# Two of four weight sums ahead of the gating in each feed-forward block, and four moves of order, in a hand-ordered fp32 kernel of two transformer blocks

## The chip, the cores and the metric

The kernel runs on one core of a Trainium2 chip. The metric is the device time of one launch in microseconds, measured on the chip. All inputs, weights and outputs are fp32; TensorE runs its matmuls on fp32 data.

## What is computed

Batch 1, 256 tokens, width 1024. The first block is a swiglu feed-forward (2816 wide, added with a gate and a factor of a half), a mixer of differential attention and an mLSTM, and a second swiglu feed-forward. The second block is a gated deltanet layer (8 heads of 128), then a layer of native sparse attention (NSA, 16 heads of 64) on keys and values shared across heads, and a last norm. Each stage is modulated by columns computed from a vector c. Cut to what matters here:

```python
def swiglu(u, w_gate, w_up, w_down):
    return (jax.nn.silu(u @ w_gate) * (u @ w_up)) @ w_down

# first block, after ada modulation of each norm:
h = h + FFN_RES * gt1[:, None, :] * swiglu(u, w1_gate[l], w1_up[l], w1_down[l])
...
q = jnp.einsum('bshd,hde->bhse', xch, w_mq)      # mLSTM
k = jnp.einsum('bshd,hde->bhse', xch, w_mk)
...
merged = jax.nn.sigmoid(ga) * (ya @ w_proj_a[l]) + jax.nn.sigmoid(gb) * (yb @ w_proj_b[l])
h = h + gt2[:, None, :] * (merged @ w_out[l])
...
h = h + FFN_RES * gt3[:, None, :] * swiglu(u, w2_gate[l], w2_up[l], w2_down[l])

# gated deltanet layer:
k = l2norm(k)                                    # sums of squares over 128 channels
decay = jnp.where(incl, jnp.exp(jnp.where(incl, diff, 0.0)), 0.0)

# NSA layer:
s_c = jnp.einsum('bghqd,bgcd->bghqc', qb, k_cmp).astype(jnp.float32) + dense_bias(d_c)
y = jnp.sum(gates[..., None].astype(o.dtype) * o * jax.nn.silu(z), axis=2)
```

## The kernel before, in words

The kernel is one program written by hand, `build()`, with one function for each engine (`tensor`, `vector`, `scalar`, `gpsimd` and one for SyncE). No scheduler sets the order: each function lists the steps of its engine in the order in which the engine runs them, and the engines meet by counting semaphores. `pe.up(name)` counts a result of TensorE under a name and `pe.at(name)` waits for it; `dve`, `act`, `pool` and a set for the transfers work in the same way. A `Ring` is a set of buffers used in turn: `open` gives the next buffer with what has to be waited for before it is written, `close` says which result frees it. PSUM has eight banks; in most stages banks 0 to 2 form the ring L, 3 and 4 the ring S and 5 to 7 the ring X. Weights come through the ring W of four slots in SBUF, fetched by SyncE in the order in which its function lists them.

All arithmetic lines of the profile are those of thin helpers: L189 matmul, L192 transpose, L195 activation (ScalarE), L198 tensor_tensor, L201 tensor_scalar, L204 scalar_tensor_tensor, L207 the custom multiply-and-sum, L222 memset, L225 DMA. So a row is told from another by its engine, its shape and the names of its tiles: `slots` are weights, `arena` is a large common region, `U`, `ABT`, `tmpA` and `x` are activations or sums over them, `tmps` are small buffers, `ps` is PSUM, `mods` are the modulation columns.

**The feed-forward blocks.** Gate and up weights come in blocks of 256 columns, 0 to 10. Blocks 5 to 10 of the first feed-forward (f1) and 1 to 10 of the second (f2) are done with seven products of half size in the place of eight (Strassen's scheme, Winograd's form), which needs sums over the weights, over the activations and over the results. `v_t(e, f, b)` (L1043) makes four sums t1 to t4 over the weights of block b on VectorE. `t_gu` (L1057) runs the products on TensorE in the order p1, p2, p6, p5, p7, p3, p4; p6 and p5 want t2 and a sum over activations, p7 wants t3 and the bank that ScalarE's copy u2 empties. ScalarE (`s_gu_blocks`, L3743) runs for block b: the copy s1 of block b, the tanh of block b - 1, and the copies u2, s5, u3, c21 of block b. The tanh waits for VectorE's sums of results of block b - 1, which are made by `v_gu` (L1132: c1 and c22). `v_gu_act` (L1151) does the gating of a block: two instructions that turn the tanh and the two results into the activation that the down projection reads, and free the rings EG and XG of two buffers each. `v_gu_blocks` (L3444) sets VectorE's order: the gating of block b - 1, the four sums of block b + 1, chunks of modulation, the sums of results of block b. In block 10 there are no weight sums left; the sums over gated values (`v_sd`) and the first sums of the down projection stand there.

**Chunks of modulation.** Modulation columns are made on VectorE by a multiply-and-sum over rows that come in chunks of 128 by 1024 into the ring AR of four buffers. `v_ada_chunks` runs one instruction for each chunk, and the table `CHUNKS` (L485) says how many chunks are taken in which block; SyncE's fetches follow the same table.

**The gated deltanet layer.** TensorE sums the squares of keys in rows; ScalarE's `s_qk_rows` (L2294) copies the rows out of PSUM into `tmps`, TensorE transposes them (L192) and sums on. `s_d_exp` runs the exponentials of the decay of a group of heads, two instructions of 256 and two of 128 columns for each group, behind VectorE's sums of a bias row that comes by DMA.

**The NSA layer.** Before the loop over scores, `t_linear` makes z for n = 0 and 1 in banks of L (each is turned into a silu by ScalarE and VectorE's scalar_tensor_tensor). In the loop, z halves use the ring LZ of two banks and scores the ring PS of four. TensorE waits before the loop for the bank of L that PS takes over, and inside it for the bank that LZ takes over.

**The bias rows.** `p_bias_rows` (L1313) on GpSimd spreads the rows of the bias over 128 copies in DRAM, in two transfers of 1536 KB. They are read in the NSA layer. In the `gpsimd` function they stand before the rotations of q and k (`p_rotate`), behind the wait for the first product of xm 1, one of the seven-product units of the mixer's input projection (in their order: xm 1, va, ga, gb, op, then pa and pb, the projections `w_proj_a` and `w_proj_b`). `p_ml_in` brings gate rows of the mLSTM, `p_merge` adds the two branches.

## Time and profile before

| | |
|---|---|
| median of 3 runs | 1186.77 us (1186.38 to 1187.87) |
| the profiled execution's own time | 1185.74 us |
| its span on the core | 1183.9 us |
| granted clock of TensorE, mean | 0.998 of full speed |
| TensorE, matmuls in flight | 1167.5 us (99%) |
| TensorE, weight loads | 1078.0 us (91%) |
| VectorE | 737.2 us (62%) |
| ScalarE | 351.4 us (30%) |
| GpSimd | 85.3 us (7%) |
| moved by DMA | 241.78 MB, mean 204 GB/s |

The span is what the profiler saw of the core from the first to the last instruction; the time of the same run is 1.8 us longer. TensorE has two rows: PE, the matmuls, and PEld, the weight loads that run beside them. In both a row groups instructions of one kind that follow one another, with the idle time before the first of them in brackets and what ended it. An idle engine costs time only where TensorE waits for it.

### The profile page before, as it was taken

Reading aid. Unit: us, or ns where it says so; the run is one execution under the profiler, and the core shown is the slowest. Engines: PE = TensorE matmul, PEld = TensorE weight load, DVE = VectorE, ACT = ScalarE, POOL = GpSimd, SP = SyncE. Lnnn points to the kernel's source line nnn. Section 1 sums busy time; section 2 is a strip of 40 time slices with the busy share of each in tenths; the row PEclk is TensorE's granted clock in tenths of the full one; section 3 lists DMA queues with packets and bytes.
Section 4 is the critical chain, followed back from the end, with each engine's and each line's share of the span. In section 5 each row is a group of like instructions: output and inputs, shape, how many; then the busy total and the mean of one; then the engine's idle time right before and its main releaser. Section 6 shows DMA issues by size and latency. Waiting matters only on the chain.

```text
span 1183.9 us, 21320 instructions
## 1 busy us (share of the span) xinstructions
PE 1167.5 (99%) x8862; PEld 1078.0 (91%) x8862; DVE 737.2 (62%) x1658; ACT 351.4 (30%) x996; POOL 85.3 (7%) x104
## 2 busy tenths in 40 slices
PE   9999999999999999999999999999999999999997
PEld 7889999998878999999999999988888998888887
DVE  4458888576048866972898878467845231167632
ACT  2111110232133555212321210245323431056542
POOL 0000000200011000021000000310004010000111
PEclk9999999999999999999999999999999999999999
DMA  9968949884555454677599739574524643642311
GB/s 343 363 214 302 331 145 303 291 307 148 202 192 186 151 214 175 223 264 234 168 362 312 269 132 302 182 269 158 142 64 143 214 143 113 194 127 73 113 66 37
DMA packets 164272, 241.78 MB, mean 204 GB/s; under 512 B 14033, under 2 KB 112559, under 8 KB 164176
## 3 DMA queue, kind: packets, MB, share of 16 engines
q1 hardware_dynamic: 156256, 230.45, 57.5%
q10 hardware_dynamic: 6784, 5.74, 1.6%
q0 software_dynamic: 1136, 4.22, 1.0%
q8 instruction: 70, 1.15, 0.4%
q14 instruction: 26, 0.21, 0.1%
HBM read 236.82 MB, written 4.62 MB: 204 GB/s over the span
## 4 chain that ended last, share of the span: by engine, by line
PE 85%; DVE 8%; DMA 3%; ACT 2%; issue 1%; POOL 0%; DVEq 0%; SPq 0%; ACTq 0%
PE ps L189 83%; DVE arena L198 3%; PE ps L192 2%; DMA slots<-in_w_mk 1%; DVE x L198 1%; DVE tmps L204 1%; ACT U L195 1%; DVE arena L207 1%; DMA slots<-in_w_proj_b 1%; ACT tmps L195 1%; DVE slots L198 0%; DMA bias_row<-rows 0%; DVE arena L204 0%; DVE slots L207 0%; ACT arena L195 0%
## 5 line engine op out<-in xcount | busy, mean ns | idle before, releaser
L189 PE MATMUL ps<-U,slots 128*128 128x128 f32 (+2 forms) x2800 | 478.9, 330 | 0.0
L189 PEld LDWEIGHTS ps<-U,slots 128*128 128x128 f32 (+1 forms) x2800 | 419.9, 190 | 40.5 <-issue 4.7
L189 PE MATMUL ps<-arena,slots 128*128 128x128 f32 (+1 forms) x1776 | 237.7, 294 | 0.9 <-DMA slots<-in_w_mk 0.9
L189 PEld LDWEIGHTS ps<-arena,slots 128*128 128x128 f32 x1776 | 225.4, 192 | 9.7 <-DMA slots<-in_w_mk 1.1
L195 ACT ACTIVATE tmps<-ps 128x256 f32<-128x256 f32 (+2 forms) x151 | 57.2, 382 | 342.6 <-PE ps L189 319.9
L207 DVE CUSTOM_DVE_ANT_0 arena<-arena,tmpA 128x1024 f32<-128x1024 f32 x96 | 118.0, 1272 | 17.0 <-DMA arena<-in_w_adaT 16.7
L195 ACT ACTIVATE arena<-ps 128x256 f32<-128x256 f32 (+3 forms) x150 | 59.3, 416 | 157.7 <-PE ps L189 153.9
L189 PE MATMUL ps<-arena 128*128 128x128 f32 (+7 forms) x940 | 101.9, 287 | 2.4 <-DVE arena L222 1.5
L189 PEld LDWEIGHTS ps<-arena 128*128 128x128 f32 (+2 forms) x940 | 92.5, 181 | 11.3 <-issue 3.7
L189 PE MATMUL ps<-ABT,arena 128*128 128x128 f32 (+5 forms) x752 | 81.9, 271 | 0.0
L189 PEld LDWEIGHTS ps<-ABT,arena 128*128 128x128 f32 (+3 forms) x752 | 72.5, 174 | 0.8 <-issue 0.8
L198 DVE TENSOR_TENSOR arena<-slots,arena 128x1024 f32<-128x1024 f32 (+1 forms) x44 | 58.6, 1331 | 0.6
L195 ACT ACTIVATE arena<-arena,st 128x128 f32<-128x128 f32 (+2 forms) x128 | 48.5, 403 | 35.2 <-DVE st L201 33.0
L189 PE MATMUL ps<-tmpA,slots 128*128 128x128 f32 x432 | 52.7, 275 | 0.0
L189 PEld LDWEIGHTS ps<-tmpA,slots 128*128 128x128 f32 x432 | 50.4, 192 | 0.0
L189 PE MATMUL ps<-x 128*128 128x128 f32 (+1 forms) x384 | 48.5, 284 | 0.6 <-DVE x L198 0.4
L204 DVE SCALAR_TENSOR_TENSOR tmps<-arena,hw,tmps 128x256 f32<-128x256 f32 x96 | 46.5, 485 | 3.4
L189 PEld LDWEIGHTS ps<-x 128*128 128x128 f32 x384 | 46.3, 192 | 1.8 <-DVE x L198 0.9
L189 PE MATMUL ps<-U,arena 128*128 128x128 f32 (+1 forms) x320 | 46.3, 296 | 0.0
L198 DVE TENSOR_TENSOR slots<-slots 128x1024 f32<-128x1024 f32 (+1 forms) x35 | 45.1, 1290 | 0.4
L195 ACT ACTIVATE U<-U,mods,sm 128x128 f32<-128x128 f32 (+1 forms) x72 | 30.3, 494 | 46.6 <-DVE sm L204 32.3
L189 PEld LDWEIGHTS ps<-U,arena 128*128 128x128 f32 x320 | 42.0, 192 | 1.6
(199 smaller groups left out, 1143.0 us busy)
## 6 DMA issues: line engine op xcount, KB each, us to landing
slots<-in_w_in SPq DMA_DIRECT2D x14, 2048.0 KB, 11.3
slots<-in_w_down SPq DMA_DIRECT2D x16, 1408.0 KB, 9.4
slots<-in_w_gate SPq DMA_DIRECT2D x18, 1024.0 KB, 8.5
slots<-in_w_up SPq DMA_DIRECT2D x18, 1024.0 KB, 11.1
arena<-in_w_adaT SPq DMA_DIRECT2D x36, 512.0 KB, 6.9
arena<-in_ada_w1T SPq DMA_DIRECT2D x24, 512.0 KB, 6.6
slots<-in_a_in_w SPq DMA_DIRECT2D x6, 2048.0 KB, 9.9
slots<-in_b_in_w SPq DMA_DIRECT2D x12, 1024.0 KB, 5.3
```

Of the source, the lines that this page charges most:

```text
L189: return Nothing() if self.e is None else self.e.matmul(*a, **k)
L192: return Nothing() if self.e is None else self.e.transpose(*a, **k)
L195: return Nothing() if self.e is None else self.e.activation(*a, **k)
L198: return Nothing() if self.e is None else self.e.tensor_tensor(*a, **k)
L204: return Nothing() if self.e is None else self.e.scalar_tensor_tensor(out=o, in0=i0, scalar=s, in1=i1, op0=op0, op1=op1)
L207: return Nothing() if self.e is None else self.e.tensor_tensor_reduce(*a)
```

## The change

Five edits, none of which adds or removes an instruction:

1. `v_t` takes a further argument `gated`. With it, the gating of that block is run between t2 and t3. `v_gu_blocks` passes block b - 1 while it makes the sums of block b + 1, so in blocks 6 to 9 of f1 and 2 to 9 of f2 the two gating instructions go from ahead of the four sums to between the second and the third. The first of the seven-product blocks has nothing to gate, and block 10 keeps its order.
2. The table `CHUNKS["f2"]` gives block 1 two chunks in the place of four, and block 9, which had none, two. The number of chunks is the same.
3. In the NSA layer the ring LZ takes banks 2 and 1 in the place of 2 and 0, and the ring PS bank 0 in the place of 1. The two waits follow.
4. ScalarE copies the rows of the keys' squares before the exponentials of the first group of decays, which stood ahead of it.
5. GpSimd issues the two copies of bias rows after the gate rows of the mLSTM, behind a wait for the first product of op 0, and no longer before the rotations.

```diff
--- before.py
+++ after.py
@@ -484,7 +484,7 @@
         AR = ring(*[arena[:, 5632 + 1024 * i:6656 + 1024 * i] for i in range(4)])
         CHUNKS = {"f1": {}, "f2": {}}
         for f, g0, counts in (("f1", 4, {4: 3, 5: 3, 6: 3, 7: 3, 8: 2, 9: 2}),
-                              ("f2", 18, {0: 3, 1: 4, 2: 3, 3: 3, 4: 3, 5: 3, 6: 3, 7: 3, 8: 3})):
+                              ("f2", 18, {0: 3, 1: 2, 2: 3, 3: 3, 4: 3, 5: 3, 6: 3, 7: 3, 8: 3, 9: 2})):
             n = 0
             for b, m in counts.items():
                 CHUNKS[f][b] = [(g0 + i // 4, i % 4) for i in range(n, n + m)]
@@ -1040,7 +1040,7 @@
             e.wait_ge(*dve.now())
             e.tensor_tensor(SU[3], a12, SU[1], ALU.subtract).then_inc(*dve.up("su", f))
 
-        def v_t(e, f, b):
+        def v_t(e, f, b, gated=None):
 
             t, free = TG.open(f, b)
             for x in free:
@@ -1050,6 +1050,8 @@
             e.tensor_tensor(t[:, 0], w[:, :, 0:4, P:T], w[:, :, 0:4, 0:P], ALU.subtract).then_inc(*dve.up(f, "t1", b))
             e.wait_ge(*dve.at(f, "t1", b))
             e.tensor_tensor(t[:, 1], w[:, :, 4:8, P:T], t[:, 0], ALU.subtract).then_inc(*dve.up(f, "t2", b))
+            if gated is not None:
+                v_gu_act(e, f, gated)
             e.tensor_tensor(w[:, :, 0:4, P:T], w[:, :, 4:8, P:T], w[:, :, 0:4, P:T], ALU.subtract).then_inc(*dve.up(f, "t3", b))
             e.wait_ge(*dve.at(f, "t2", b))
             e.tensor_tensor(t[:, 2], w[:, :, 4:8, 0:P], t[:, 1], ALU.subtract).then_inc(*dve.up(f, "t4", b))
@@ -2960,8 +2962,8 @@
 
 
         m15 = C("m15")
-        LZ = ring(banks[2][:, :], banks[0][:, :])
-        PS = ring(*[banks[b][:, :] for b in (3, 4, 5, 1)])
+        LZ = ring(banks[2][:, :], banks[1][:, :])
+        PS = ring(*[banks[b][:, :] for b in (3, 4, 5, 0)])
         EE = ring(B(0)[:, 0:816], B(0)[:, 816:1632], arena[:, 8 * UNIT + 1240:8 * UNIT + 2056], arena[:, 20384:21200])
         EA = ring(tmpA[:, :, :].rearrange("p i n -> p (i n)")[:, 0:1024], ABT[:, :, :].rearrange("p i n -> p (i n)")[:, 0:1024])
         ES = ring(*[st[:, i, :] for i in range(4)])
@@ -3402,12 +3404,12 @@
             t_cmp3(e, 1)
             for n in range(2):
                 t_linear(e, "z", n, U, u_in("n5"), 256, ("z", n))
-            for x in free_of(L, 1) + free_of(X):
+            for x in free_of(L, 0) + free_of(X):
                 e.wait_ge(*x)
             for t in range(10):
                 if t < 8:
                     t_na_scores(e, t)
-                for x in free_of(L, (2, 0)[t]) if t < 2 else ():
+                for x in free_of(L, (2, 1)[t]) if t < 2 else ():
                     e.wait_ge(*x)
                 if t < 9:
                     t_z_half(e, ZIN[t][0], 0)
@@ -3444,11 +3446,10 @@
         def v_gu_blocks(e, f, b0):
 
             for b in range(b0, 11):
-                if b > b0:
+                if b < 10:
+                    v_t(e, f, b + 1, b - 1 if b > b0 else None)
+                else:
                     v_gu_act(e, f, b - 1)
-                if b < 10:
-                    v_t(e, f, b + 1)
-                else:
                     v_sd(e, f, 0, 9)
                     v_dn_t1(e, f, 0)
                     v_dn_t2(e, f, 0)
@@ -3878,8 +3879,8 @@
             s_decay_in(e)
             s_conv(e, "dc", 15)
             s_qk_squares(e, 7)
+            s_qk_rows(e, "k", 7)
             s_d_exp(e, 0)
-            s_qk_rows(e, "k", 7)
             s_d_exp(e, 1)
             s_d_exp(e, 2)
             s_silu(e, "zg", 0)
@@ -3971,8 +3972,6 @@
         def gpsimd(e):
             p_bias(e)
             p_squares(e, "n2")
-            e.wait_ge(*pe.at("7", "p1", "xm", 1))
-            p_bias_rows(e)
             for pair in range(4):
                 p_rotate(e, "q", pair)
                 p_rotate(e, "k", pair)
@@ -3982,6 +3981,8 @@
                     for h in range(3):
                         p_ml_in(e, h)
             p_ml_in(e, 3)
+            e.wait_ge(*pe.at("7", "p1", "op", 0))
+            p_bias_rows(e)
             for b in range(2):
                 for half in range(2):
                     p_merge(e, b, half)
```

VectorE in the second feed-forward, from the chunks of block 1 on. The `L207` pairs are chunks, `tmps<-ps,tmps` and `tmps<-tmps,rstd` are the sums of results, `tmps<-tmps` and `arena<-tmps` the gating, and the rows with `slots` the weight sums t1 to t4. Before:

```order
L207 ISA arena,mods<-arena,tmpA 128x1024 [waits s_ada_chunk0]
L207 ISA mods 128x1
L207 ISA arena,mods<-arena,tmpA 128x1024 [waits s_ada_chunk1]
L207 ISA mods 128x1
L207 ISA arena,mods<-arena,tmpA 128x1024 [waits s_ada_chunk2]
L207 ISA mods 128x1
L198 TENSOR_TENSOR tmps<-ps,tmps 128x512 [waits s_products,s_scalar_results]
L198 TENSOR_TENSOR tmps<-tmps,rstd 128x2x128 [waits s_scalar_results]
L204 SCALAR_TENSOR_TENSOR tmps<-tmps 128x512 [waits s_scalar_results]
L198 TENSOR_TENSOR arena<-tmps 128x2x2x128 [waits s_vector_results]
L198 TENSOR_TENSOR arena<-slots 128x1024 [waits s_slot0,s_products]
L198 TENSOR_TENSOR arena<-slots,arena 128x1024 [waits s_vector_results]
```

Now:

```order
L207 ISA arena,mods<-arena,tmpA 128x1024 [waits s_ada_chunk0]
L207 ISA mods 128x1
L198 TENSOR_TENSOR tmps<-ps,tmps 128x512 [waits s_products,s_scalar_results]
L198 TENSOR_TENSOR tmps<-tmps,rstd 128x2x128 [waits s_scalar_results]
L198 TENSOR_TENSOR arena<-slots 128x1024 [waits s_slot0,s_products]
L198 TENSOR_TENSOR arena<-slots,arena 128x1024 [waits s_vector_results]
L204 SCALAR_TENSOR_TENSOR tmps<-tmps 128x512 [waits s_scalar_results]
L198 TENSOR_TENSOR arena<-tmps 128x2x2x128 [waits s_vector_results]
L198 TENSOR_TENSOR slots<-slots 128x2x4x128
L198 TENSOR_TENSOR arena<-slots,arena 128x1024
```

Two chunks are gone from ahead of the sums of results of block 1, and t1 and t2 of the next block stand ahead of the gating.

ScalarE in the gated deltanet layer, one piece of the difference (`arena<-arena,gates` are the exponentials, `tmps<-ps 128x128` is the copy of the rows):

```order
-L195 ACTIVATE arena<-arena,gates 128x256
-L195 ACTIVATE arena<-arena,gates 128x128
-L195 ACTIVATE arena<-arena,gates 128x256
-L195 ACTIVATE arena<-arena,gates 128x128
 L195 ACTIVATE tmps<-ps 128x128
+L195 ACTIVATE arena<-arena,gates 128x256
+L195 ACTIVATE arena<-arena,gates 128x128
+L195 ACTIVATE arena<-arena,gates 128x256
+L195 ACTIVATE arena<-arena,gates 128x128
```

The copy now stands ahead of the four exponentials of the first group.

GpSimd in the mixer, the end of its part, one piece of the difference (`arena<-tmps,arena` are rotations, `tmps<-blocks` the gate rows of the last head, `arena<-arena` the merges; the `+` row had stood ahead of the first rotation):

```order
 L198 TENSOR_TENSOR arena<-tmps,arena 128x512 x2
 L225 DMA tmps<-blocks 128x256
+L225 DMA bias_rows<-bias_row 128x8x384 x2
 L198 TENSOR_TENSOR arena<-arena 128x4x128 x4
 L225 DMA tmpA<-in_c_rows 128x1024
```

The two transfers of bias rows now follow the last gate rows and stand ahead of the merges.

## Rows read from the trace of the kernel before

**Rows 1.** The page: busy us (share of the span) and instructions of each engine.

```profile
PE 1167.5 (99%) x8862; PEld 1078.0 (91%) x8862; DVE 737.2 (62%) x1658; ACT 351.4 (30%) x996; POOL 85.3 (7%) x104
```

**Rows 2.** TensorE's waits by what ended them: us in total, times, longest.

```profile
PE ps L189 <- ACT tmps L195: 2.1, 2, 1.4
PE ps L189 <- DVE arena L222: 1.5, 1, 1.5
PE ps L192 <- ACT tmps L195: 1.2, 1, 1.2
...
PE ps L189 <- DMA slots<-in_w_mk: 0.9, 1, 0.9
```

**Rows 3.** Timeline, feed-forward blocks: start us, us, engine and line, [idle before <-releaser].

```profile
104.66 0.69 DVE L204 SCALAR_TENSOR_TENSOR tmps<-tmps 128x512 f32<-128x512 f32 x1 [2.33 <-ACT tmps L195]
...
169.62 1.53 PEld L189 LDWEIGHTS ps<-arena 128*128 128x128 f32 x13 [0.66 <-DVE arena L198]
...
604.56 0.69 DVE L204 SCALAR_TENSOR_TENSOR tmps<-tmps 128x512 f32<-128x512 f32 x1 [0.70 <-ACT tmps L195]
605.89 1.22 DVE L198 TENSOR_TENSOR arena<-slots 128x1024 f32<-128x1024 f32 x1
...
611.73 0.38 ACT L195 ACTIVATE tmps<-ps 128x256 f32<-128x256 f32 x1 [3.19 <-PE ps L189]
```

**Rows 4.** Timeline, second feed-forward, end of block 1 and block 2.

```profile
590.35 1.22 DVE L207 CUSTOM_DVE_ANT_0 arena<-arena,tmpA 128x1024 f32<-128x1024 f32 x1
...
591.49 0.69 DVE L198 TENSOR_TENSOR tmps<-ps,tmps 128x512 f32<-128x512 f32 x1
...
592.55 0.63 ACT L195 ACTIVATE tmps<-tmps 128x512 f32<-128x512 f32 x1 [5.29 <-DVE tmps L198]
...
593.56 1.86 PEld L189 LDWEIGHTS ps<-ABT,slots 128*128 128x128 f32 x16 [1.61 <-issue]
```

**Rows 5.** Timeline, gated deltanet layer, sums of the keys' squares.

```profile
812.94 1.59 PEld L189 LDWEIGHTS ps<-U,slots 128*128 128x128 f32 x8 [0.20 <-issue]
...
813.29 3.28 DVE L198 TENSOR_TENSOR arena<-arena,cst 128x256 f32<-128x256 f32 x6 [2.29 <-DMA arena<-bias_row]
814.48 1.49 ACT L195 ACTIVATE arena<-arena,gates 128x256 f32<-128x256 f32 x4 [2.46 <-DVE arena L198]
...
816.18 0.14 PEld L192 LDWEIGHTS ps<-cst,tmps 128*128 128x128 f32 x1 [1.65 <-ACT tmps L195]
```

**Rows 6.** Timeline, NSA layer, last products before the score loop.

```profile
1026.63 0.69 DVE L204 SCALAR_TENSOR_TENSOR arena<-tmps,ps 128x512 f32<-128x512 f32 x1 [7.51 <-ACT tmps L195]
...
1033.53 0.69 DVE L204 SCALAR_TENSOR_TENSOR arena<-tmps,ps 128x512 f32<-128x512 f32 x1 [6.22 <-ACT tmps L195]
...
1034.27 1.62 PEld L189 LDWEIGHTS ps<-arena 64*128 64x128 f32 x16 [1.87 <-DVE arena L222]
```

**Rows 7.** Timeline of the mixer's first products, and the answer on in_w_mk.

```profile
253.16 0.94 POOL L225 DMA_DIRECT2D bias_rows<-bias_row  x1 [14.50 <-PE ps L189]
...
264.46 3.32 PEld L189 LDWEIGHTS ps<-arena,slots 128*128 128x128 f32 x16 [1.09 <-DMA slots<-in_w_mk]
...
264.55 0.90 POOL L225 DMA_DIRECT2D bias_rows<-bias_row  x1 [10.46 <-issue]
...
DMA to landing us min/median/max: 12.9/12.9/12.9
```

**Rows 8.** Around op 0: timeline, a stretch (busy, clock, DMA share, GB/s), in_w_proj_a.

```profile
449.93 0.38 ACT L195 ACTIVATE arena<-ps 128x256 f32<-128x256 f32 x1 [2.71 <-PE ps L189]
...
458.00:461.00 3.00, 3.00 (x30) 3.00 (x29) 2.90 (x4) 1.16 (x6) 0.00 (x0) 1.00 0.00 0
...
L225 SPq DMA_DIRECT2D slots<-in_w_proj_a x2: 368/475/582, 464.1 to 464.5; - x2
...
DMA to landing us min/median/max: 7.8/10.3/12.8
...
473.98 1.22 DVE L198 TENSOR_TENSOR x<-slots 128x1024 f32<-128x1024 f32 x1
```

## The prediction

> **What bounds the kernel now.** I read the page's busy times first [rows 1]. TensorE has matmuls in flight for 1167.5 of 1183.9 us, so only what shortens TensorE's own sequence, or a wait in front of it, can move the end. VectorE has 62% and the transfers idle stretches; both matter only where TensorE waits for them. Next the list of TensorE's waits [rows 2]: all of them together are about 10 us, so that is the most that a change of order can return. Four of the lines are the targets: ScalarE's copies once for 1.4 us, a memset of VectorE for 1.5, ScalarE before a transpose (L192) for 1.2, the transfer of w_mk for 0.9. Then I took each place on the timeline, with the idle time before the weight load there, because that is the other half of TensorE.
>
> The clock is no term: the profiled run was granted 0.998 of full speed, and no instruction is added or taken away.
>
> **Edit 1, sums before the gating, twelve blocks: 0 us.** The order rows show t1 and t2 of the next block ahead of the two gating instructions. In the blocks of the first feed-forward VectorE stood idle 2.33 us for tanh [rows 3], in the early ones of the second 0.70 [rows 3]; the two sums, 1.22 us each, now fill that time. VectorE gains up to 2.3 us in each of twelve blocks. But TensorE does not wait for VectorE in these blocks: the list of waits has one stall on the copies behind tanh (edit 2's), and the tail of each block row, where TensorE waits 0.66 us for the sums over the gated values [rows 3], is made by block 10, whose order the change leaves alone. The new price is that the gating ends later by what the sums exceed the idle time, at most 2.44 - 0.70 = 1.7 us, and holds its two buffers for that long. The gating of a block ended at 605.9 and ScalarE's first copy that writes into the same ring ran at 611.73 [rows 3], so 5.8 us of slack cover it. The last two sums were behind the gating before too; they never come later. Below, I bound this edit by 0 and by the rival that takes that cover away.
>
> **Edit 2, two chunks from block 1 of the second feed-forward to block 9: 1.5 us.** VectorE takes four chunks of the modulation before it can form the sums of results of block 1, the first of which starts at 591.49 [rows 4]. ScalarE's tanh at 592.55 waits for them, its two copies (results of block 2 that have to leave their bank) stand behind the tanh, and TensorE's product with the weights in the slots waits for a copy: 1.61 us by the weight load [rows 4], 1.4 by the matmul [rows 2]. The last chunk starts at 590.35 and the sums at 591.49 [rows 4], so a chunk costs 1.14 us, and two fewer (the order rows) put everything 2.3 us earlier, which is more than the stall. The stall goes; the midpoint of 1.4 and 1.61 is 1.5. What is late next there is TensorE itself. Block 9 gets the two chunks: blocks 2 to 8 carry three each, and the list of waits holds no second stall of that kind in them, so a block with two does not stall either. SyncE's fetches follow the same table; the first fetch of the down weights now stands behind two more chunks in its queue, and it is wanted only in block 10. I cost that at nothing.
>
> **Edit 4, the copy of the rows of squares before the decay exponentials: 1.4 us.** TensorE's sixteen narrow products end at 812.94 [rows 5]. ScalarE then waits for VectorE, which itself waits 2.29 us for a transfer of the bias row [rows 5], runs four activations at 814.48, and only then copies the rows that TensorE transposes at 816.18, 1.65 us late by the weight load [rows 5] and 1.2 by the matmul [rows 2]. Moved ahead, the copy runs as soon as the narrow products are done, about 813, long before TensorE has finished its eight wide products. The exponentials start after it at their old time, since they wait for VectorE. Some gap remains, as 0.20 before the load at 812.94 shows [rows 5]: bounds 1.2 and 1.65, and 1.4 in between.
>
> **Edit 3, the third bank, swapped with the first: 1.7 us.** Before the score loop TensorE waits until the bank of the scores is free. That was the bank of the second silu of z, whose last instruction ran at 1033.53; now it is the first one's, at 1026.63 [rows 6]. TensorE started its scores at 1034.27, 1.87 us late by the weight load [rows 6], 1.5 by the matmul [rows 2]. (The page names a memset as releaser; it is the next instruction on VectorE, and the release is inferred.) The bank that is needed 7 us later is then waited for inside the loop, behind products that take TensorE at least as long as the 1.87 us that are missing. Bounds 1.5 and 1.87, midpoint 1.7.
>
> **Edit 5, the two large copies of bias rows moved from the mixer's first products to after op 0: 1.0 us, less 0.2.** GpSimd issued the first at 253.16 [rows 7], just behind SyncE's fetch of w_mk, whose landing took 12.9 us; the load that needs it began 1.09 us late [rows 7], 0.9 by the matmul [rows 2]. Without the copies it has to land only 1.1 us sooner; the first half of w_proj_a, which met nothing, landed in 7.8 [rows 8]. Midpoint 1.0. Behind the old wait on GpSimd's queue stood the rotations of q and k, now free to go sooner. Behind the new one stand only the merges, far later. At the new place, the wait is for the first product of op 0, whose result ScalarE copies at 449.93 [rows 8], so the first copy goes out near 450 and the second, if as far behind it as before (264.55 less 253.16 [rows 7], 11.4 us), near 461. The transfers are idle there: 0.00 in 458 to 461 [rows 8]. But w_proj_a is fetched at 464.1 [rows 8] and lands at 471.9, 2.1 us before VectorE reads it at 473.98 [rows 8]. If the second copy ends near 470 it shares some 5 us with that fetch and, at half the rate, costs it 2.5 us, 0.4 beyond the slack. Bounds of this cost: 0, and 3.0 if the landing takes the 12.9 us of w_mk (464.1 + 12.9 = 477.0 against 473.98). I take 0.2, near the low end, since the overlap is partial.
>
> DMA: Bandwidth & Descriptors, a page of the Trainium skill, says in its section on queues, rings and completion order that each transfer engine takes turns between the queues that have work, packet by packet. The trace agrees as far as w_mk goes (12.9 us for its landing beside the copies). Taken alone, the rule gives the 2.5 us above.
>
> **Sum.** 1.5 + 1.4 + 1.7 + 1.0 - 0.2 = 5.4 us. By matmul idle the four are 1.4 + 1.5 + 1.2 + 0.9 = 5.0, by weight loads 1.61 + 1.65 + 1.87 + 1.09 = 6.2. The span goes from 1183.9 to 1178.5, its run from 1185.74 to 1180.3. That run is 1.0 below the median of the three, so against 1186.77 the forecast is 1181.4.
>
> Perfetto Trace Analysis, also of the Trainium skill, holds in its section on the most-contended engine that matmul busy time is no good measure of TensorE and the busy share of weight loads is. By it the sum would be 6.2 - 0.2 = 6.0, and the time 1180.8.
>
> **Rivals.**
> B: **w_proj_a comes 1 to 3 us late** because of the second copy. VectorE is nearly full from there on, so its delay reaches TensorE. For it: the 12.9 us of w_mk. Against: a slack of 2.1 us and idle transfers before 464. It gives back 1 to 3 us of 5.6: about 1183.2. Chance 0.12.
> C: **the waits return in another form, or part of the change does not do what it says**: the copy that was moved waits for a buffer, the bank is held by something else, w_mk is late anyway. For it: the releasers are inferred, and the memset in the list of waits [rows 2] might be the true one. If the two largest go unreturned (1.5 + 1.7) the gain is 2.2, the time 1184.6. Chance 0.09.
> D, slower: **the delayed gating stalls TensorE in every block.** It decides if the gating's buffers are wanted as soon as they were freed, that is if the 5.8 us of slack are less than 1.7. Then eight blocks of the second feed-forward pay up to 1.7 us and the four of the first 2.44 - 2.33 = 0.1: 14.0 us, less the 5.4: 1195.4. Against it: ScalarE's row at 611.73. Chance 0.03.
>
> **Numbers.** The likeliest case (0.76) gives 1181.4. I call 0.2%, 2.4 us, what can be told from no change. Faster by more: the likeliest case, most of B and a third of C: 0.87. Same: the rest of B and C: 0.10. Slower: 0.03. The low end takes 6.2 from the lowest run, 1186.38, and 0.6 for the small stalls in [rows 2] that a less loaded VectorE could lift: 1179.6. The high end holds C with the scatter of the runs: 1185.2.
>
> **What the profile would show.** Right: no gap before the weight loads at the four places (264.5, 593.6, 816.2 and 1034.3, each now earlier by what was gained before it) beyond some 0.2 to 0.3; idle time of VectorE before the gating gone, with TensorE's 0.66 us tails unchanged; the sums of block 1 near 588.2 (591.49 less two chunks and the 1.0 gained at w_mk); the two copies of bias rows near 449 and 460; and VectorE reading w_proj_a without a wait. Wrong: a wait of VectorE on w_proj_a (B), a wait of TensorE behind ScalarE or VectorE at one of the four places (C), or small stalls repeated 12.5 us apart in the feed-forward (D).

## The result, and the profile after

| | before | changed |
|---|---|---|
| median of 6 runs | 1186.3 us (1183.76 to 1187.87) | 1181.79 us (1179.26 to 1182.83) |
| the profiled execution's own time | 1185.74 us | 1181.78 us |
| its span | 1183.9 us | 1179.9 us |
| granted clock of TensorE, mean | 0.998 | 0.999 |

The ratio is 0.9963, with a 95% interval of 0.9953 to 0.9973: 4.5 us or 0.37% faster. (Three more runs of the kernel before moved its median from 1186.77 to 1186.3.)

The page of the changed kernel, busy times. It answers to [rows 1]:

```profile
PE 1167.2 (99%) x8862; PEld 1078.0 (91%) x8862; DVE 738.1 (63%) x1658; ACT 352.2 (30%) x996; POOL 86.0 (7%) x104
```

No engine does less or more. Of TensorE's waits in the changed kernel (us in total, times, longest), this line matters. It answers to [rows 2]:

```profile
PE ps L189 <- DVE x L198: 1.9, 2, 1.3
```

All four lines of [rows 2] that the edits were aimed at are gone or reduced: the memset, the transpose behind ScalarE, the transfer of w_mk, and the larger of the two waits on ScalarE's copies. But a wait on VectorE's sums over `x` has grown from 0.4 to 1.9 us, 1.3 of it at one place. TensorE's two waits on `arena`, 0.5 us each by the matmul, are the tails of the feed-forwards, as before.

Where did the time go? The start times of the same instructions in both traces tell it, place by place. Here are TensorE's first product of U with a weight slot, and six of its weight loads. Each load but the last stands behind a stretch whose waits one of the edits 2 to 5 was to change. The kernel before:

```profile
18.65 1.67 PE L189 MATMUL ps<-U,slots 128*128 128x256 f32 x7
...
308.37 1.59 PEld L189 LDWEIGHTS ps<-slots,arena 128*128 128x128 f32 x8 [0.88 <-ACT arena L195]
...
561.28 0.30 PEld L189 LDWEIGHTS ps<-arena,cst 128*128 128x128 f32 x2 [0.54 <-POOL arena L198]
...
704.63 4.99 PEld L189 LDWEIGHTS ps<-arena 128*128 128x128 f32 x44 [0.67 <-DVE arena L198]
...
852.76 1.94 PEld L189 LDWEIGHTS ps<-arena 64*64 64x64 f32 x64 [0.33 <-issue]
...
1060.20 1.62 PEld L189 LDWEIGHTS ps<-arena 64*128 64x128 f32 x16 [0.33 <-issue]
...
1177.68 0.30 PEld L189 LDWEIGHTS ps<-tmps,cst 128*128 128x128 f32 x2 [0.81 <-ACT tmps L195]
```

The changed kernel:

```profile
19.21 1.03 PE L189 MATMUL ps<-U,slots 128*128 128x256 f32 x4
...
307.68 1.59 PEld L189 LDWEIGHTS ps<-slots,arena 128*128 128x128 f32 x8 [0.88 <-ACT arena L195]
...
561.92 0.30 PEld L189 LDWEIGHTS ps<-arena,cst 128*128 128x128 f32 x2 [0.55 <-POOL arena L198]
...
703.58 4.99 PEld L189 LDWEIGHTS ps<-arena 128*128 128x128 f32 x44 [0.67 <-DVE arena L198]
...
850.25 1.94 PEld L189 LDWEIGHTS ps<-arena 64*64 64x64 f32 x64 [0.33 <-issue]
...
1056.15 1.62 PEld L189 LDWEIGHTS ps<-arena 64*128 64x128 f32 x16 [0.33 <-issue]
...
1173.63 0.30 PEld L189 LDWEIGHTS ps<-tmps,cst 128*128 128x128 f32 x2 [0.81 <-ACT tmps L195]
```

Taking differences from row to row:

| stretch | shift at its end | so the stretch changed by | what is in it |
|---|---|---|---|
| up to the first product | +0.56 | +0.56 | nothing of the change |
| to 308 | -0.69 | -1.25 | w_mk, no longer beside the bias rows |
| to 562 | +0.64 | +1.33 | op 0, w_proj_a, w_proj_b |
| to 704 | -1.05 | -1.69 | second feed-forward |
| to 851 | -2.51 | -1.46 | rows of squares |
| to 1058 | -4.05 | -1.54 | banks |
| to 1175 | -4.05 | 0 | |

Without the start, in which nothing was changed, the kernel gained 1.25 + 1.69 + 1.46 + 1.54 = 5.94 us, gave back 1.33, and came out 4.6 us ahead: that is the measured 4.5.

The first line of that table needs a word, because it decides how a single run can be read. TensorE's first product with the weights starts at 18.65 us in one profile and at 19.21 in the other. Over the 14 profiles of this study it starts between 16.92 and 19.31 us, in kernels that are the same up to there. The profiles fall into two groups, five at 16.92 to 17.22 us and nine at 18.62 to 19.31, so a difference of two medians can hold some 2 us of this. So below each kernel is compared by its span less that start ("the rest"): 1165.25 us before, 1160.69 changed.

The landing of `in_w_mk` and the four places in the changed kernel. They answer to [rows 4 to 7]:

```profile
DMA to landing us min/median/max: 9.2/9.2/9.2
...
263.77 0.30 PEld L189 LDWEIGHTS ps<-arena,slots 128*128 128x128 f32 x2
...
589.84 0.69 DVE L198 TENSOR_TENSOR tmps<-ps,tmps 128x512 f32<-128x512 f32 x1
...
592.51 0.64 PEld L189 LDWEIGHTS ps<-ABT,slots 128*128 128x128 f32 x5
...
812.03 0.28 ACT L195 ACTIVATE tmps<-ps 128x128 f32<-128x128 f32 x1 [0.98 <-PE ps L189]
...
813.51 0.14 PEld L192 LDWEIGHTS ps<-cst,tmps 128*128 128x128 f32 x1
...
1030.22 0.95 PEld L189 LDWEIGHTS ps<-arena 64*128 64x128 f32 x10 [0.33 <-issue]
```

w_mk lands in 9.2 us in the place of 12.9, and the load that needs it has no idle time ahead of it. In the second feed-forward the sums of results of block 1 are formed at 589.84, and the load at 592.51 has no gap. The forecast was 588.2; with the 0.64 us by which this trace runs late there (table), 591.49 less two chunks makes 589.85. ScalarE copies the rows at 812.03, and the transpose's load at 813.51 has none either. The scores' load keeps 0.33 us.

The new wait. In the changed kernel GpSimd's copies, the answer on `in_w_proj_a` (its issues, its landing), and the rows of VectorE and TensorE behind it. They answer to [rows 8]:

```profile
449.50 0.93 POOL L225 DMA_DIRECT2D bias_rows<-bias_row  x1 [47.35 <-PE ps L189]
...
459.54 0.90 POOL L225 DMA_DIRECT2D bias_rows<-bias_row  x1 [9.11 <-issue]
...
L225 SPq DMA_DIRECT2D slots<-in_w_proj_a x2: 368/475/582, 463.4 to 463.8; - x2
...
DMA to landing us min/median/max: 11.0/13.5/16.0
...
474.45 1.23 DVE L198 TENSOR_TENSOR x<-slots 128x1024 f32<-128x1024 f32 x1 [1.07 <-DMA slots<-in_w_proj_a]
...
480.79 1.30 PEld L189 LDWEIGHTS ps<-x 128*128 128x128 f32 x11 [1.49 <-DVE x L198]
```

The first copy goes out at 449.50 and the second at 459.54, within half a microsecond of the places that the forecast named for the profile (449 and 460). The second lands 9.5 us after its issue, at 469.0. w_proj_a is fetched at 463.4 and lands in 11.0 us in the place of 7.8. VectorE waits 1.07 us for it, and the weight load behind it shows 1.49 us of idle time where the kernel before had 0.33. The share of the transfer engines from 461 on (busy of each engine, clock, DMA share, GB/s), 0.02 and 0.42 in the kernel before:

```profile
461.00:464.00 3.00, 3.00 (x29) 3.00 (x29) 3.00 (x5) 0.47 (x2) 0.00 (x0) 1.00 0.84 304
...
464.00:467.00 3.00, 3.00 (x29) 3.00 (x29) 0.79 (x5) 2.90 (x4) 0.00 (x0) 1.00 1.00 243
```

VectorE in the first feed-forward, changed kernel. These answer to the first row of [rows 3]:

```profile
104.55 1.22 DVE L198 TENSOR_TENSOR arena<-slots 128x1024 f32<-128x1024 f32 x1 [1.65 <-DMA slots<-in_w_up]
...
130.31 0.69 DVE L204 SCALAR_TENSOR_TENSOR tmps<-tmps 128x512 f32<-128x512 f32 x1 [0.50 <-ACT tmps L195]
...
138.15 0.69 DVE L198 TENSOR_TENSOR tmps<-ps,tmps 128x512 f32<-128x512 f32 x1 [1.86 <-PE ps L189]
...
155.32 0.69 DVE L204 SCALAR_TENSOR_TENSOR tmps<-tmps 128x512 f32<-128x512 f32 x1 [3.65 <-ACT tmps L195]
```

The idle time of 2.33 us ahead of the gating has fallen to 0.50 or less in these blocks, and it is back in other places: 1.65 us ahead of the first weight sum, which now comes before the weights have landed, or 0.66 us behind TensorE, and up to 1.86 us ahead of the sums of results. At the end of block 9 VectorE stands idle for 3.65 us, 0.68 more than before. VectorE finished earlier and then waited for TensorE; inside the blocks TensorE's weight loads show no idle time at all.

### The profile page after: what moved, and what is told of

The parts are those of the page before. It is cut to its first block, busy times and chain, and to the rows that moved or that the text cites. A ratio compares the mean times of both kernels' runs of the same rounds, so it can differ in the third digit from the quotient of the medians.

```text
span 1179.9 us, 21319 instructions
## 1 busy us (share of the span) xinstructions
PE 1167.2 (99%) x8862; PEld 1078.0 (91%) x8862; DVE 738.1 (63%) x1658; ACT 352.2 (30%) x996; POOL 86.0 (7%) x104
## 3 DMA queue, kind: packets, MB, share of 16 engines
q8 instruction: 70, 1.15, 0.4%
## 4 chain that ended last, share of the span: by engine, by line
PE 92%; DVE 4%; ACT 1%; issue 1%; DMA 1%; POOL 0%; DVEq 0%; ACTq 0%
PE ps L189 90%; PE ps L192 2%; DVE arena L198 2%; DMA slots<-in_w_proj_b 1%; DVE x L198 1%; ACT U L195 1%; ACT tmps L195 0%; DVE slots L207 0%; DVE arena L204 0%; DVE rstd L216 0%; DVE tmps L204 0%; DVE slots L198 0%; DVE tmps L198 0%; ACT arena L195 0%; POOL arena L198 0%
## 5 line engine op out<-in xcount | busy, mean ns | idle before, releaser
L207 DVE CUSTOM_DVE_ANT_0 arena<-arena,tmpA 128x1024 f32<-128x1024 f32 x96 | 118.2, 1274 | 15.3 <-DMA arena<-in_w_adaT 15.0
```

Of the source, the lines that this page charges most:

```text
L207: return Nothing() if self.e is None else self.e.tensor_tensor_reduce(*a)
```

## The experiments

Theory after the result: the four waits are gone, edit 1 does nothing for the time, and the second copy of bias rows delays w_proj_a by 3.2 us, 1.1 of which VectorE and then TensorE pay. Rivals: the reordering of edit 1 carries part of the gain; VectorE is late near 480 us for work of its own; one of the four waits had another cause than the one read off the trace. All twelve kernels change only the order or the place of work.

| kernel | span | first product | the rest | against before | ratio, 95% interval |
|---|---|---|---|---|---|
| before | 1183.9 | 18.65 | 1165.25 | | |
| changed | 1179.9 | 19.21 | 1160.69 | -4.56 | 0.9963, 0.9953 to 0.9973 |
| sums only | 1184.1 | 18.82 | 1165.28 | +0.03 | 1.0002, 0.9993 to 1.0011 |
| without the sums | 1179.4 | 18.62 | 1160.78 | -4.47 | 0.9958, 0.9943 to 0.9973 |
| copies as before | 1179.4 | 18.62 | 1160.78 | -4.47 | 0.9964, 0.9950 to 0.9977 |
| copies behind w_mk | 1176.6 | 17.02 | 1159.58 | -5.67 | 0.9945, 0.9933 to 0.9958 |
| one copy at each place | 1176.1 | 17.09 | 1159.01 | -6.24 | |
| chunks 2 and 2 only | 1180.4 | 16.92 | 1163.48 | -1.77 | |
| chunks 3 and 1 only | 1181.5 | 17.22 | 1164.28 | -0.97 | |
| banks only | 1182.3 | 19.31 | 1162.99 | -2.26 | |
| rows only | 1182.9 | 18.84 | 1164.06 | -1.19 | |
| gating behind four sums | 1177.2 | 17.19 | 1160.01 | -5.24 | |
| gating behind the chunks | 1179.5 | 18.97 | 1160.53 | -4.72 | |
| copies behind w_mk, tails | 1177.0 | 18.84 | 1158.16 | -7.09 | 0.9932, 0.9918 to 0.9945 |

Kernels without a ratio were run once. The places where a transfer decides vary between profiles of kernels that are alike there. The gap before the load that waits for w_proj_b's sums (near 507 us) is 0.23 to 1.07 us in the seven kernels with the copies at their first place. The one near 480 us is 0.77, 1.49, 1.56 and 2.12 us in the four with both copies behind op 0. So a difference in the rest of less than about 1 us says nothing by itself; the gap at the place in question does.

**Sums only.** Edit 1 alone, on the kernel before:

```diff
-                if b > b0:
-                    v_gu_act(e, f, b - 1)
                 if b < 10:
-                    v_t(e, f, b + 1)
+                    v_t(e, f, b + 1, b - 1 if b > b0 else None)
                 else:
+                    v_gu_act(e, f, b - 1)
```

> The kernel before with edit 1 alone. Theory (TensorE never waits for the gating or the weight sums inside the blocks): no change, ratio 1.000 within 0.001; VectorE's idle time before the gating falls from 2.3 and 0.7 us to near 0 where tanh comes in time, TensorE's stall in block 2 of the second feed-forward stays at 1.6 us (weight load), the two tails stay at 0.66. Rival 1 (the reordering itself brings the gain of the second feed-forward): the stall in block 2 is gone and the ratio is near 0.9986. Rival 2 (the delayed gating holds its buffers): stalls of up to 1.7 us repeated 12.5 us apart, ratio above 1.002.

Measured: 1185.83 against 1185.56 us, ratio 1.0002 (0.9993 to 1.0011). TensorE's load in block 2 of the second feed-forward, in this kernel:

```profile
593.71 1.86 PEld L189 LDWEIGHTS ps<-ABT,slots 128*128 128x128 f32 x16 [1.61 <-issue]
```

Both tails show 0.67. The stall stays: the reordering brings nothing by itself, and the interval leaves at most 0.8 us to it. Rivals 1 and 2 fall.

**Without the sums.** Edits 2 to 5:

```diff
+                if b > b0:
+                    v_gu_act(e, f, b - 1)
                 if b < 10:
-                    v_t(e, f, b + 1, b - 1 if b > b0 else None)
+                    v_t(e, f, b + 1)
                 else:
-                    v_gu_act(e, f, b - 1)
```

> The changed kernel without edit 1 (edits 2 to 5 stay). Theory: the stall in block 2 stays away, so the gain of the second feed-forward (1.7 us) is the chunks' alone. One small loss: block 9 now has two chunks (2.3 us) where VectorE had 1.75 us to spare, so its sums come some 0.5 us late and the tail of the second feed-forward waits 1.1 to 1.3 us in the place of 0.67. Ratio to the kernel before 0.996 to 0.997. Rival (edit 1 carries the blocks): a stall of over 1 us in a block, or the tail at 2 us or more, ratio 0.998.

Measured: 1181.12 us, ratio 0.9958 (0.9943 to 0.9973), the same as the changed kernel. Two weight loads of TensorE, near op 0 and at the tail of the second feed-forward:

```profile
480.83 3.65 PEld L189 LDWEIGHTS ps<-x 128*128 128x128 f32 x32 [2.12 <-DVE x L198]
...
703.11 4.99 PEld L189 LDWEIGHTS ps<-arena 128*128 128x128 f32 x44 [0.67 <-DVE arena L198]
```

The theory's main part held: no stall in the blocks. Its small part missed. The tail waits 0.67 us, as always, and not 1.1 to 1.3. The likely reason, read from ScalarE's order and not tried by itself, is that the tanh of block 9 stands behind ScalarE's first copy of block 10, which waits for TensorE, so that 0.5 us of VectorE do not reach it. So edit 1 is not even needed to make room for edit 2. The wait near 480 us is 2.12 us here, against 1.49 in the changed kernel, with w_proj_a landing in 11.7 us; the gap near 507 us is 0.25 against 0.77, so that the two nearly cancel in the rest. The overlap of two transfers has no fixed price.

**Copies behind w_mk.** The changed kernel, with the wait and the two copies moved:

```diff
             p_squares(e, "n2")
+            e.wait_ge(*pe.at("mk", 0))
+            p_bias_rows(e)
             for pair in range(4):
...
             p_ml_in(e, 3)
-            e.wait_ge(*pe.at("7", "p1", "op", 0))
-            p_bias_rows(e)
```

> The changed kernel with the two copies of bias rows issued behind the first product with w_mk (about 267 us), where the transfers of the changed kernel are idle up to 285 us, in the place of behind op 0. Theory (the copies delay w_proj_a, and that is what TensorE's wait of 1.3 us near 480 us is): w_proj_a lands in about 8 us again, VectorE does not wait for it, TensorE's gap near 480 us falls from 1.49 to 0.33 us, w_mk stays unhindered; 1.2 to 1.3 us less than the changed kernel, ratio to before about 0.995. Rival 1 (VectorE is late near 480 us for its own work): the gap stays over 1 us. Rival 2 (the second copy now delays the next fetches of w_in): a new wait near 300 us.

Measured: 1178.41 us against 1185.56, ratio 0.9945 (0.9933 to 0.9958). GpSimd's issues, w_proj_a's landing, and a load of TensorE:

```profile
L225 POOL DMA_DIRECT2D bias_rows<-bias_row x2: 902/922/942, 265.6 to 275.2; - x2
...
DMA to landing us min/median/max: 7.9/10.4/12.9
...
477.43 2.75 PEld L189 LDWEIGHTS ps<-x 128*128 128x128 f32 x24 [0.33 <-DVE x L198]
```

The copies went out at 265.6 and 275.2, w_proj_a landed in 7.9, and the gap near 480 us fell to 0.33, what it is in the kernel before. No new wait came near 300 us. The rest of the span is 1.11 us shorter than the changed kernel's; two gaps account for it: 1.49 to 0.33 near 480 us, and 0.77 to 0.85 at the load of 504.68, where VectorE waits for w_proj_b. The medians differ by more, 7.15 us from the kernel before where the rest says 5.67: this kernel's median run is of the group that starts early (17.02 us against 18.65). Rival 1 falls: VectorE had no work of its own that was late. The intervals of the two ratios overlap, so that this kernel is faster than the changed one rests on the traces.

**Copies as before.** Edits 1 to 4, the copies at their first place:

```diff
             p_squares(e, "n2")
+            e.wait_ge(*pe.at("7", "p1", "xm", 1))
+            p_bias_rows(e)
             for pair in range(4):
...
-            e.wait_ge(*pe.at("7", "p1", "op", 0))
-            p_bias_rows(e)
```

> The changed kernel without edit 5 (copies of bias rows at their old place). Theory (edit 5 trades one wait for another): the gap of 1.1 us before the load that needs w_mk is back, the one near 480 us falls from 1.49 to 0.33, so the time is that of the changed kernel within 0.3 us, ratio to before about 0.996. Rival (edit 5 is worth its 1.0 us): 1 us more than the changed kernel.

Measured: 1181.3 us, ratio 0.9964 (0.9950 to 0.9977), the changed kernel's. The load that needs w_mk, and the one near 480 us:

```profile
264.37 3.32 PEld L189 LDWEIGHTS ps<-arena,slots 128*128 128x128 f32 x16 [1.11 <-DMA slots<-in_w_mk]
...
480.22 3.65 PEld L189 LDWEIGHTS ps<-x 128*128 128x128 f32 x32 [0.33 <-DVE x L198]
```

The 1.1 us are back and the gap near 480 us is at 0.33 again. As the theory has it, edit 5 as made is worth nothing: it trades 1.1 us at w_mk for 1.2 at w_proj_a.

**One copy at each place.** The first copy behind w_mk, the second alone behind op 0:

```diff
+            e.wait_ge(*pe.at("mk", 0))
+            p_bias_rows(e, (0,))
...
             e.wait_ge(*pe.at("7", "p1", "op", 0))
-            p_bias_rows(e)
+            p_bias_rows(e, (8,))
```

> The changed kernel with the first copy of bias rows behind the first product with w_mk and the second alone behind op 0. It tells which of the two is in the way of w_proj_a. Theory (the second, because it goes out 10 us after the first and is still moving at 463): a lone copy sent near 449 has landed by 459, w_proj_a lands in about 8 us and TensorE's gap near 480 is 0.33. Rival (any copy at that place is enough): the gap stays over 1 us.

Measured: 1177.95 us in one run. Issues, and w_proj_a's landing:

```profile
L225 POOL DMA_DIRECT2D bias_rows<-bias_row x2: 919/930/942, 265.7 to 447.5; - x2
...
DMA to landing us min/median/max: 7.7/10.2/12.7
```

A lone copy sent at 447.5 is out of the way, w_proj_a lands in 7.7, and the gap near 480 us is 0.33. So it is the second copy, 10 us behind the first, that collided.

**Chunks 2 and 2 only, and chunks 3 and 1 only.** Edit 2 alone is in the diff of the change; half of it is:

```diff
-                              ("f2", 18, {0: 3, 1: 4, 2: 3, 3: 3, 4: 3, 5: 3, 6: 3, 7: 3, 8: 3})):
+                              ("f2", 18, {0: 3, 1: 3, 2: 3, 3: 3, 4: 3, 5: 3, 6: 3, 7: 3, 8: 3, 9: 1})):
```

> The kernel before with edit 2 alone. Theory (four chunks ahead of block 1's sums of results make ScalarE's copies late): the gap of 1.61 us before the weight load of block 2 near 592 us is gone, nothing else moves, span 1.6 us shorter. Rival (it takes edit 1 as well): a gap of over 0.5 us stays there, or one comes in block 9 or 10.

> The kernel before with three chunks in block 1 and one in block 9. A chunk is 1.14 us of VectorE, so if the stall is the chunks' time, the gap of 1.61 us falls by 1.14 to about 0.5. If it goes at once to none, the stall has a second cause; if it stays near 1.6, the chunks are not the cause.

The load of block 2 with two chunks fewer:

```profile
589.85 1.87 PEld L189 LDWEIGHTS ps<-ABT,slots 128*128 128x128 f32 x16
```

With one fewer:

```profile
591.36 1.86 PEld L189 LDWEIGHTS ps<-ABT,slots 128*128 128x128 f32 x16 [0.46 <-issue]
```

The gap went from 1.61 to 0.46 and to none: 1.15 us for the first chunk, which is the 1.14 that a chunk takes. The rests, 0.97 and 1.77 us shorter, agree within the scatter near 507 us (gaps of 1.07 and 0.56 here, 0.61 in the kernel before).

**Banks only.** Edit 3 alone:

```diff
-        LZ = ring(banks[2][:, :], banks[0][:, :])
-        PS = ring(*[banks[b][:, :] for b in (3, 4, 5, 1)])
+        LZ = ring(banks[2][:, :], banks[1][:, :])
+        PS = ring(*[banks[b][:, :] for b in (3, 4, 5, 0)])
```

> The kernel before with edit 3 alone. Theory (the wait is for the bank of the second silu, released at 1034.2): the gap before the scores falls from 1.87 to 0.33 us, 1.54 less. Rival (the memset that the profile names is what TensorE waits for): the gap stays at 1.87.

TensorE's load and VectorE's memset in this kernel:

```profile
1032.66 1.62 PEld L189 LDWEIGHTS ps<-arena 64*128 64x128 f32 x16 [0.33 <-issue]
...
1034.10 0.18 DVE L222 MEMSET arena<- 128x25 f32 x4
```

The scores' load runs at 1032.66, ahead of the memset at 1034.10, so TensorE never waited for the memset that the profile names; it waited for the instruction before it. The gap is 0.33, as expected. (The rest of the span is 2.26 us shorter, more than 1.54: the gaps at w_mk, at the rows' transpose and near 507 us were 0.1, 0.2 and 0.4 us smaller in this profile, the last 0.23 against 0.61.)

**Rows only.** Edit 4 alone:

```diff
             s_qk_squares(e, 7)
+            s_qk_rows(e, "k", 7)
             s_d_exp(e, 0)
-            s_qk_rows(e, "k", 7)
```

> The kernel before with edit 4 alone. Theory: ScalarE's copy of the rows runs right behind the narrow products, near 813 us, the gap of 1.65 us before the transpose falls to 0.2, 1.45 less, and the exponentials start when they did. Rival (the copy waits for its buffer): a gap of over 0.5 stays.

The narrow products, ScalarE's copy and the transpose's load:

```profile
812.78 0.64 PE L189 MATMUL ps<-tmps,cst 128*32 128x128 f32 x16
...
813.49 0.28 ACT L195 ACTIVATE tmps<-ps 128x128 f32<-128x128 f32 x1 [1.08 <-PE ps L189]
...
814.97 0.14 PEld L192 LDWEIGHTS ps<-cst,tmps 128*128 128x128 f32 x1
```

The copy starts within 0.1 us of the end of the narrow products (813.42), and the load has no gap. The rest is 1.19 us shorter, 0.26 less than expected; TensorE's wait at w_mk was 0.2 us longer in this profile and the gap near 507 us 0.15.

**Gating behind four sums, gating behind the chunks.** The changed kernel with the gating moved further back, to see where the cover of edit 1 ends:

```diff
-                    v_t(e, f, b + 1, b - 1 if b > b0 else None)
+                    v_t(e, f, b + 1)
+                    if b > b0:
+                        v_gu_act(e, f, b - 1)
```

and, for the second, the last two of these lines behind `v_ada_chunks` (in blocks up to 9).

> The changed kernel with the gating behind all four weight sums, not behind two. It then ends 4 x 1.22 - 0.70 = 4.2 us later than in the kernel before in the early blocks of the second feed-forward. If the slack of 5.8 us read off the trace is right, TensorE shows no stall in the blocks and the span stays that of the changed kernel within 0.5 us. Rival (the slack is less): stalls of up to 4.2 us, 12.5 us apart.

> The changed kernel with the gating behind the four sums and the block's chunks (3 x 1.14 us), so up to 4.2 + 3.4 = 7.6 us later than before, 1.8 more than the slack of 5.8. If the slack is right and the ring is what decides, ScalarE's first copy of a block waits for VectorE and TensorE shows small stalls in the early blocks of the second feed-forward, at most 1.8 us each, 12.5 apart, so 0 to 9 us in all. If there is no wait of ScalarE at all the slack was read too small.

Behind the sums: rest 1160.01 us, no stall in the blocks. (It is 0.68 us less than the changed kernel's because the gap near 480 us is 0.77 and not 1.49.) Behind the chunks: rest 1160.53, no stall in the blocks either, but ScalarE's first copy of block 3 now waits for the gating, by the timeline of ScalarE. Below it the first copy of block 4 in the kernel before:

```profile
600.18 0.38 ACT L195 ACTIVATE tmps<-ps 128x256 f32<-128x256 f32 x1 [1.96 <-DVE arena L198]
...
613.58 0.38 ACT L195 ACTIVATE tmps<-ps 128x256 f32<-128x256 f32 x1 [1.46 <-PE ps L189]
```

So the ring does decide there, at one block. Of the 1.96 us, 1.46 stand before this copy in the other blocks too, where it waits for TensorE; the late gating adds 0.50. None of it reaches TensorE. The forecast had 1.8 us (7.6 less 5.8), because the slack of 5.8 us was read at the wrong copy. The row at 611.73 [rows 3] is the last copy of block 3, into buffers that the block already holds. The copy that needs the buffers of the gating that ended at 605.9 is the first of block 4, at 613.58: 7.7 us of slack, and that is ScalarE's. The point from which rival D would decide lies further out than either kernel reached.

**Copies behind w_mk, tails.** What remains are the tails. VectorE is idle for 3.65 us ahead of the gating of block 9, and the first sum of the down weights can be made there:

```diff
                 else:
+                    v_dn_t1(e, f, 0)
                     v_gu_act(e, f, b - 1)
                     v_sd(e, f, 0, 9)
-                    v_dn_t1(e, f, 0)
                     v_dn_t2(e, f, 0)
```

> The changed kernel with the copies of bias rows behind the first product with w_mk, and in block 10 of both feed-forwards the first sum of down weights (1.62 us) ahead of the gating of block 9, where VectorE stands idle 3.65 us for tanh. Theory: the tails' stalls of 0.67 us by the weight load fall to 0.2 or less, 0.9 to 1.0 us in all, on top of the copies' 1.2; ratio to before 0.994, about 1 us less than the kernel with the copies alone. Rival (the down weights have not landed yet, or ScalarE sets the tail): the tails keep their 0.67.

Measured: 1178.29 us against 1185.95, ratio 0.9932 (0.9918 to 0.9945). The sum, the gating, and TensorE's load at the first tail:

```profile
151.96 1.62 DVE L198 TENSOR_TENSOR arena<-slots 128x1408 f32<-128x1408 f32 x1 [0.67 <-PE ps L189]
...
154.94 0.69 DVE L204 SCALAR_TENSOR_TENSOR tmps<-tmps 128x512 f32<-128x512 f32 x1 [1.36 <-ACT tmps L195]
...
169.06 2.09 PEld L189 LDWEIGHTS ps<-arena 128*128 128x128 f32 x18
```

The sum stands in the idle time, and the load that waited 0.67 us has no gap. The second tail has none either. The rest of the span is 1158.16 us, 1.4 less than with the copies moved alone and 2.5 less than the changed kernel's; its interval lies below the changed kernel's. This is the fastest version of the study.

## Why the prediction was right, and where it was off

The forecast was 1181.4 us, between 1179.6 and 1185.2; measured were 1181.79. Direction and size held, and so did the mechanism of the four waits. The one new wait was put at 0.2 us and cost 1.33.

- **Edit 1, 0 us.** Right: ratio 1.0002 alone, and the changed kernel without it is as fast. The reason given was right too, TensorE does not wait for VectorE in the blocks. What the text said beside it, that VectorE gains up to 2.3 us a block, was wrong: VectorE's idle time moved behind the weights and behind TensorE, it did not go. The slack of 5.8 us was read at the wrong copy; it is 7.7 us, which makes rival D less likely still.
- **Edit 2, 1.5 us forecast, 1.69 measured.** The mechanism is shown by the steps of 1.15 us a chunk.
- **Edit 4, 1.4 forecast, 1.46 measured.** The idle time before the load, 1.65 us, went to none, but not all of it was won: in the kernel before the transpose's load and its matmul both start at 816.18, in the changed one the load starts at 813.51 and the matmul 0.21 us later. (The 812.94 that the forecast gives as the end of the narrow products is the start of the next load; they end at 813.01.)
- **Edit 3, 1.7 forecast, 1.54 measured.** The term was oversized by the idle time that stays there when nothing is waited for: 1.87 - 0.33 = 1.54. The load there has another shape (64 rows) than the one before it; the same 0.33 us stands near 480 us between loads of one shape, so what makes it is open. I had such an allowance in the text for edit 4 and left it out here.
- **w_mk, 1.0 forecast, 1.25 measured** over the stretch, of which the trace's gap explains 1.09. The forecast set w_mk's 12.9 us beside the 7.8 of w_proj_a, a transfer of twice the size; without the copies beside it w_mk lands in 9.2 to 9.6 us (seven profiles), so the copies cost its landing 3.3 to 3.7 us.
- **The cost at w_proj_a, 0.2 forecast, 1.33 measured.** This is the step that failed, and it is rival B, to which I gave 0.12: w_proj_a came 3.2 us later after its fetch, VectorE waited for it, and the delay reached TensorE. The place of the second copy was right (459.54), the slack of 2.1 us too: w_proj_a was wanted at 473.38 and fetched at 463.39. What failed was the size. At half the rate over 5 us I made the delay 2.5 us and the excess 0.4, and then took 0.2, below my own estimate. In the four profiles with both copies behind op 0 the second copy and w_proj_a overlap by 4.9, 5.4, 5.6 and 6.3 us (from the fetch to the copy's landing), and the landing grew by 2.5, 3.3, 3.2 and 3.9 us against the 7.8 of the kernel before: 0.5 to 0.6 of the overlap. In the changed kernel's profile VectorE's wait of 1.07 us reached TensorE whole (0.33 to 1.49), and VectorE's rows show no idle time between that wait and the sum that TensorE reads. The cost was 0.44 us in the mildest of the four and 1.79 in the worst, so the 1.33 is one draw.
- **Matmul or weight load.** The four gains add up to 5.94 us. Idle time before the weight loads gave 6.2, idle time before the matmuls 5.0. The page Perfetto Trace Analysis of the Trainium skill (section on the most-contended engine) trusts weight loads over matmul busy time. It speaks of shares of the whole span; carried over to single stalls, as the forecast did, it gives a sum 0.3 us too high here, against 0.9 too low by the matmuls. With the 0.33 us that stay at the banks taken off it is 5.9.

Two errors of opposite sign, 0.3 too little for the four waits and 1.1 too little for the new one, left the sum 0.8 us off. The time came out closer, 0.4 us off, by luck: the forecast was counted from 1186.77, and with six runs the median before is 1186.3. The rivals C (waits return in another form) and D (the delayed gating) did not happen.

## What to carry to other kernels

Price a stall of TensorE by the idle time before its weight load, less what stays there when nothing is waited for (here up to 0.33 us). Before a bulk transfer is moved to an idle stretch, follow it to its end and past it: what matters is not whether the queues are idle when it starts but which fetch with little slack starts before it ends, and how much later it lands (here 0.5 to 0.6 of the overlap). Reordering an engine that nobody waits for moves its idle time; look for the one place where somebody does (here the tails), and use the idle time there.

## What the runs showed that was not expected

- The first product with the weights starts at 16.92 to 19.31 us in kernels that are the same up to there, more than half of what the whole change brings. The groups part before anything with weights: the same four products of a row start at 4.03 us in all 14 profiles and take 3.78 us in the nine late ones, 2.07 to 2.36 in the five early ones. Here the kernel before and the copies behind w_mk:

```profile
4.03 3.78 PE L189 MATMUL ps<-rows 1*128 1x512 f32 x4
...
4.03 2.15 PE L189 MATMUL ps<-rows 1*128 1x512 f32 x4
```

  The granted clock reads 1.00 in both from 4 to 7 us, and 0.50 (1.2 GHz) from 8 to 11 us in the early one alone, which stays ahead all the same; so this column does not tell them apart. What does is open.
- GpSimd's second copy of 1536 KB left 9.1 us after the first had been issued (10.46 in the kernel before), though no wait stands between them in the program; the profile puts the time down to the issue. It leaves when the first has landed. In the 13 profiles in which the two follow each other, the second issue starts 0.3 to 0.5 us after the landing of the first (changed kernel: 449.50 and 9.6 us to landing, then 459.54; before: 253.16 and 11.1, then 264.55). This is what puts the second copy beside w_proj_a; a second copy that goes out at once was not seen.
- The releaser that the profile names can be the instruction next to the true one: the memset of [rows 2] was not waited for.
